# Chunked recurrence of a two-block transformer: the level products and their masked copies go over half of the columns

## The reference, cut to what matters

```python
def step(s, inp):
    qi, ki, vi, fi = inp
    a = jnp.cumsum(fi, axis=2)
    o_inter = jnp.einsum('bhtd,bhde->bhte', qi * jnp.exp(a), s)
    diff = a[:, :, :, None, :] - a[:, :, None, :, :]
    decay = jnp.exp(jnp.where(tri, diff, NEG_BIG))
    scores = jnp.einsum('bhtd,bhjd,bhtjd->bhtj', qi, ki, decay)
    o_intra = jnp.einsum('bhtj,bhje->bhte', scores, vi)
    ...
o_f, s_f = gla_chunk_scan(q, k_f, v, lf_f, s0_f)
o_b, s_b = gla_chunk_scan(rev(q), rev(k_b), rev(v), rev(lf_b), s0_b)
```

## Time and profile before

| | |
|---|---|
| median of 3 runs | 2542.26 us (2541.05 to 2546.97) |
| profiled execution: its own time | 2544.42 us |
| profiled execution: its span, first to last instruction | 2542.6 us |
| time around the span | 1.8 us |
| mean granted clock of TensorE | 0.990 |
| PE busy | 2449.7 us, 96% of the span |
| DVE busy | 1402.7 us, 55% |
| ACT busy | 1159.5 us, 46% |
| the recurrence, from first transposes to last `out` | about 1640 to 1964 us of the span |

### The profile page before, as it was taken

One profiled execution on the slowest core, in us unless ns is written; L12 is line 12 of the kernel. 1 busy time (PEld: TensorE's weight loads), 2 busy tenths in 40 slices (PEclk: granted clock), 3 DMA queues, 4 the chain that ended last, 5 costly groups with the idle time before them and its releaser, 6 DMA issues.

```text
span 2542.6 us, 30787 instructions
## 1 busy us (share of the span) xinstructions
PE 2449.7 (96%) x12116; PEld 1935.1 (76%) x12116; DVE 1402.7 (55%) x2264; ACT 1159.5 (46%) x1824; POOL 381.7 (15%) x307
## 2 busy tenths in 40 slices
PE   8999999999999999999999899999988998999998
PEld 6667678888877778888887677788777786788886
DVE  4787558758635456746765555354445433543443
ACT  4455654334445545434443766554555323442342
POOL 0001312112200002212212100011111211220221
PEclk9999999999999999999999999999999999899999
DMA  4122144434332224443522100110110332232331
GB/s 150 59 84 86 55 157 133 157 100 151 116 98 75 79 71 168 159 128 108 166 83 72 67 26 18 66 42 34 42 34 17 114 118 92 70 108 87 98 112 56
DMA packets 67439, 232.47 MB, mean 91 GB/s; under 512 B 7552, under 2 KB 7680, under 8 KB 66912
## 3 DMA queue, kind: packets, MB, share of 16 engines
q1 hardware_dynamic: 67296, 230.51, 28.3%
HBM read 226.21 MB, written 4.28 MB: 91 GB/s over the span
## 4 chain that ended last, share of the span: by engine, by line
PE 61%; ACT 6%; DVE 3%; issue 2%; POOL 0%; ACTq 0%; DVEq 0%
PE psum L424 17%; PE psum L426 16%; PE psum L425 16%; PE psum L2362 1%; PE psum L1004 1%; ACT SP L1052 1%; PE psum L977 1%; PE psum L1149 1%; ACT wH L409 1%; PE psum L1023 1%; PE psum L1160 1%; PE psum L1172 1%; PE psum L2329 1%; PE psum L2330 1%; DVE SP L1094 0%
## 5 line engine op out<-in xcount | busy, mean ns | idle before, releaser
L424 PE MATMUL psum<-hH,wH 128*128 128x512 f32 x1944 | 793.6, 408 | 32.8 <-DVE wL L414 10.7
L426 PE MATMUL psum<-hH,wL 128*128 128x512 f32 x1944 | 763.7, 393 | 0.0
L425 PE MATMUL psum<-hL,wH 128*128 128x512 f32 x1944 | 762.3, 392 | 0.0
L414 DVE TENSOR_TENSOR wL<-raw,wH 128x1024 fp32r<-128x1024 f32 (+2 forms) x358 | 454.2, 1269 | 456.7 <-ACT wH L409 455.9
L409 ACT ACTIVATE wH<-raw 128x1024 fp32r<-128x1024 f32 (+2 forms) x358 | 368.1, 1029 | 511.9 <-PE psum L426 510.8
L424 PEld LDWEIGHTS psum<-hH,wH 128*128 128x128 f32 x1944 | 366.7, 189 | 144.4 <-issue 41.1
L426 PEld LDWEIGHTS psum<-hH,wL 128*128 128x128 f32 x1944 | 366.8, 189 | 80.7
L425 PEld LDWEIGHTS psum<-hL,wH 128*128 128x128 f32 x1944 | 367.7, 189 | 67.7 <-issue 2.2
L424 PE MATMUL psum<-gH,wH 128*128 128x512 f32 x528 | 206.0, 390 | 0.0
L425 PE MATMUL psum<-gL,wH 128*128 128x512 f32 x528 | 205.4, 389 | 0.0
L426 PE MATMUL psum<-gH,wL 128*128 128x512 f32 x528 | 205.4, 389 | 0.0
(11 more groups left out here) (349 smaller groups left out, 3412.2 us busy)
## 6 DMA issues: line engine op xcount, KB each, us to landing
raw<-in_up SPq DMA_DIRECT2D x132, 512.0 KB, 3.4
raw<-in_dn SPq DMA_DIRECT2D x48, 704.0 KB, 4.1
raw<-in_win SPq DMA_DIRECT2D x56, 512.0 KB, 3.4
mbuf<-in_wmod SPq DMA_DIRECT2D x48, 512.0 KB, 3.5
raw<-in_we SPq DMA_DIRECT2D x33, 512.0 KB, 3.5
raw<-in_wq SPq DMA_DIRECT2D x24, 512.0 KB, 3.5
tm<-toep SPq DMA_DIRECT2D x32, 256.0 KB, 4.2
raw<-in_wo SPq DMA_DIRECT2D x32, 256.0 KB, 2.6
```

The lines of the kernel that those rows point to most:

```text
L414: ve.do.tensor_tensor(flat_of(wLb, n), flat_of(rawb, n), flat_of(wHb, n).bitcast(F), ALU.subtract).then_inc(*w_lo.up(n))
L424: pe.do.matmul(o, H[:, k, :], high(k), start=k == 0, stop=False)
L425: pe.do.matmul(o, H[:, k, :], low(k), start=False, stop=False)
L426: ins = pe.do.matmul(o, L[:, k, :], high(k), start=False, stop=k == kt - 1)
```

## The change: what it does

In `use` the moving operand is now only the query half of `Z` (`queries(...)`), 64 columns for each chunk in place of 128; the stationary operand is the whole chunk as before. The result goes densely into the first 256 columns of the bank (`half_scores(mat)`). The masked copy reads those 256 columns, and the query half of the mask, and writes into the query half of `scT`. On each of the five engines the same instructions stand in the same order, and no wait is added or removed; only these two change their shapes: PE's matmul from 128 to 64 moving columns, and DVE's masked copy from 128x512 to 128x256, in the views 4x64, 8x32, 16x16, 32x8, 64x4, 128x2 and 256 single elements. The copy of the diagonal (line 2510) stays at 128x512.

```diff
@@ pe_recurrence, "use"
                 for c in range(4):
-                    ins = pe.do.matmul(b128(pb, c), Z[z_][:, c, :], Z[z_][:, c, :], start=True, stop=True)
+
+                    ins = pe.do.matmul(half_scores(mat)[:, c, :, :], Z[z_][:, c, :], queries(Z[z_], mat, d)[:, c, :, :],
+                                       start=True, stop=True)
                 ins.then_inc(*g_pm.up((h, d, mat)))
@@ beside halves
     def halves(y, b_):
         return y.rearrange("p c (n u b) -> p c n u b", u=2, b=b_)
+
+    def queries(y, mat, d):
+
+        return halves(y, LEVELS[mat - 1])[:, :, :, (1, 0)[d], :]
+
+    def half_scores(mat):
+
+        return bank[2 + mat % 2][:, 0:256].rearrange("p (c n b) -> p c n b", c=4, b=LEVELS[mat - 1])
@@ ve_recurrence, "use"
-                ve.do.copy_predicated(scT, mask(2 * (mat - 1) + d), b3(bank[2 + mat % 2], 4)).then_inc(*g_cp.up(scored))
+                ve.do.copy_predicated(queries(scT, mat, d), queries(mask(2 * (mat - 1) + d), mat, d),
+                                      half_scores(mat)).then_inc(*g_cp.up(scored))
```

## The result

The changed kernel takes 2554.51 us (2545.73 to 2555.3, 11 runs) against 2542.6 us (2539.8 to 2546.97, 11 runs) of the kernel before, run beside it: ratio 1.0031, 95% interval 1.0018 to 1.0044, or 4.6 to 11.2 us more (the medians are 11.9 us apart, since that of the changed kernel lies in the upper of two groups). The forecast was 2540.1 us with a range of 2529 to 2548. Its times lie in two groups, 2545.7 to 2546.9 (5 runs) and 2554.5 to 2555.3 (6 runs); the profiled execution, 2554.51 us with a span of 2552.7 us, is of the upper one. The profile of before has a span of 2542.6 us, so the two traces are 10.1 us apart.

A forecast was written before the change was run, and what follows sets the result against it. PE, busy 96% of the span, was taken as the bound: its pace saves 0, eight shorter masked copies on its path save 2.2 us, so 2542.26 - 2.2 = 2540.1 us, range 2529 to 2548.

The forecast's parts named there:

- Rival C: Around PE's waits, half the columns make the granted clock fall more often, 1.7 us each, up to 2553.7 us; chance 0.09.
- 2.2 us for the copies: Path saving from 8 shorter masked copies: 1.6 us at ends of heads 0 to 2, 0.55 in head 3.
- PE's pace: In rows of eight, the weight load keeps each pair at about 0.111 us despite 64 columns; saving 0.
- Rival B: The matmul's columns set PE's pace in rows of eight: 2523.6 us, or 2530 to 2534 for paces between; chance 0.16.
- a record of about 220 ns: Sign for PE: one matmul's record some 50 ns shorter while starts stay 0.105 to 0.112 us apart.
- The masked copies: All 56 on DVE were to fall from 736 to 463 ns, alike in all seven views.
- the view of single elements: Sign against the copy estimate: masked copies in this view standing out above 600 ns.
- the whole 0.55 us goes through: At the ends of heads 0 to 2, two shorter copies ahead of `out` save 0.55 us a head.
- PE's wait ahead of `out`: Sign for the path: this wait at a head's end falls by some 0.3 us.
- the two waits with one copy of an earlier level in front: Head 3, first direction, waits at 1914.87 and 1920.62: one shorter copy each, 0.55 us saved together.
- DVE's busy time: Was to fall by about 15 us, 56 copies at 0.273 us, nearly all beside PE's projections.
- the wait of 0.74 us at 1707.03: PE's wait with one masked copy ahead of its `make`: 0.27 us shorter, giving nothing more in time.

The follow-up runs named there:

- e_prod_half: Kernel before with only the product halved to 64 moving columns, written into its places of the bank, under the whole copy: 2550.64 us, ratio 1.0034.
- e_full_dense: Changed kernel with the product over all 128 moving columns again, ordered by halves, the half copy kept: 2541.46 us, ratio 1.0001 to the kernel before.
- e_fill: Changed kernel plus ten unread matmuls of 512 columns in PE's wait at each head's start: 2543.07 us, ratio 1.0002 to the kernel before.
- e_thin_fills: Changed kernel plus unread matmuls in PE's waits, ten at each head's start and more in head 3: 2536.28 us, ratio 0.9976 to the kernel before.
- e_thin_starts: Changed kernel with 64 moving columns only in each head's first two rows, 128 by halves elsewhere: 2548.95 us, ratio 1.0022 to the kernel before.
- e_thin_end: Changed kernel with 64 moving columns only in the last four rows of head 3's second direction: 2546.84 us, ratio 1.0017 to the kernel before.
- e_stat64: Changed kernel with 64 stationary columns too, so half of the scores are not computed: one run, 2538.86 us.
- b_fill2: Kernel before plus ten unread matmuls of 512 columns ahead of each head's first product: 2539.25 us, ratio 0.9989 to the kernel before.
- e_target2: Changed kernel with 128 moving columns by halves and the copy's mask, source and target all dense, scores partly wrong: one run, 2539.63 us.
- e_copy_half: Kernel before with only the masked copy halved, the product over all 128 columns: 2543.09 us, ratio 1.0001 to the kernel before.
- e_mask_dense: Changed kernel with each mask stored by halves, so that the copy reads it densely: 2547.51 us, ratio 1.0027 to the kernel before.

## Why the prediction was wrong

**The step that failed** is the forecast's treatment of the clock. Rival C had the mechanism, the place ("with half the columns in each row of eight the array streams less just there") and the price ("each further fall costs 1.7 us", eight of them 2553.7 us); 11.9 us more loss are seven times that price, and the result is 2554.51. That its number came so near is in part luck: it counted eight new falls and took off 2.2 us for the copies, and the trace has one new fall (head 0's start), three falls of twice the length and one that is 10.2 us longer. Rival C got 0.09, by the argument "against it: the last rows of eight of a head, with short waits only, had 1.00 [...] and no wait becomes longer". Both halves of this are true and beside the point. The last rows of a head still have 1.00 (1700 to 1710 us above). No wait had to become longer: the waits of 2.5 us were there already, and three of four heads had a fall behind them. What changed is, for the most part, how long the fall lasts. The forecast asked only whether there would be more falls, priced at 1.7 us, and put the growth of those that were there at nothing; the runs show the falls of the starts of heads 1 to 3 costing 3.4 us each, and the one of head 3's end lasting from 1951 to 1969. That the product's columns cause it is shown (e_prod_half, e_full_dense), that it happens behind PE's waits too (e_fill, e_thin_fills), and that a few rows are enough (e_thin_starts, e_thin_end). How 64 columns in place of 128 keep the clock down is not shown.

**PE's pace** was right: 0.111 us a pair with 64 columns as with 128, and the load as its cause (e_stat64). Rival B is gone. The sign that was named for it, a record of about 220 ns, came only in part. One line's instructions, of the changed kernel's product (ns min/median/max):

```profile
L2363 PE MATMUL psum<-hf x256: 217/275/476, 1656.3 to 1964.0; 128*128 128x64 f32 x128
```

and of the kernel before:

```profile
L2362 PE MATMUL psum<-hf x256: 270/275/580, 1657.0 to 1957.6; 128*128 128x128 f32 x128
```

The shortest went from 270 to 217 ns, the 53 ns that the forecast gave to 64 columns; the median stays at 275: most records hold more than the time of their columns. The Trainium skill's figure of about 81 ns for a pair ("TensorE: Matmul & The Clock Gate", section "Back-to-back issue gap") was reached in no row of eight, with 128 moving columns or with 64; the trace doesn't agree.

**The masked copies** were right for levels 1 to 5 (0.44 us, forecast 0.463) and wrong for levels 6 and 7, which the forecast took to be alike since a pass of two operands over the same views takes 413 ns in the median. The prediction named the sign of it, "wrong if the view of single elements stands out above 600 ns". And just these two are on the path at each head's end. The chain of waits of the changed kernel there, which answers to the earlier trace rows:

```profile
1712.52 0.94 DVE f6r L2279
1713.46 0.66 DVE hf L2543
...
1714.21 0.74 DVE hf L2543
...
1714.99 0.49 PE psum L2371 x2
```

0.66 and 0.74 us, as they were. So "the whole 0.55 us goes through" became nothing: PE's wait ahead of `out` is 0.91 us, not 0.3 less. The periods say the same without the clock's noise: 81.97 and 82.01 in b_fill2 with whole copies and products, 82.04 in e_thin_fills with half ones. That the path was read rightly e_target2 shows. In head 3 the two waits with one copy of an earlier level in front did shorten, 1.78 and 0.66 us to 1.51 and 0.34:

```profile
1919.93 1.10 PE L2363 MATMUL psum<-ssum 128*128 128x64 f32 x8 [1.51 <-DVE ssum L2444]
...
1925.36 1.11 PE L2363 MATMUL psum<-hf 128*128 128x64 f32 x8 [0.34 <-DVE hf L2444]
```

Of the 2.2 us of the sum 0.6 were left.

**DVE's busy time** was to fall by about 15 us and fell by 5.1 (1402.7 to 1397.6). The copies gave 12.0 us (41.2 to 29.2), but the multiplications of `make` took 5.8 back. One of their two groups, of the kernel before and of the changed one:

```profile
L2434 DVE TENSOR_TENSOR ssum<-E,qt 128x256 f32<-128x256 f32 x24 | 10.5, 440 | 0.0
```

```profile
L2444 DVE TENSOR_TENSOR ssum<-E,qt 128x256 f32<-128x256 f32 x24 | 14.4, 601 | 0.0
```

The other group went from 417 to 475 ns. Behind a shorter copy DVE starts 19 of its 56 multiplications while POOL is still 0.43 to 0.56 us from the end of its own, and just these 19 take 0.71 to 0.85 us; the other 37 do not overlap POOL's and take about 0.42. Before, no overlap was over 0.26 us and none took over 0.53. The trace of e_copy_half shows the same 19. At one such place the shorter copy brings PE next to nothing: the wait of 0.74 us at 1707.03, which was to lose 0.27, became 0.68. The forecast put this lengthening at nothing. That POOL's work is the cause is read from this overlap; no run moved it.

**What stays open.** Why an execution has the long low stretch or not. The changed kernel's two groups are some 8.6 us apart, with mean clocks over the whole execution of 0.988 and 0.984; executions of before at 2546.8 to 2547.4 us were at 0.989. The heads' starts in the traces without filler and with 128 stationary columns say how far the columns settle it. With rows of 128 columns (before, e_copy_half, e_full_dense, e_thin_end, e_target2) 11 of 20 starts have a fall, ten of 3.4 us and one of 6.8. With rows of 64 (after, e_prod_half, e_thin_starts, e_mask_dense) 14 of 16 have one, nine of 6.8 us and five of 3.4; the fall at head 0's start is one of 3.4 us in all four. So thin rows make the long fall common and are neither enough for it nor needed. What decides within one kernel was not tried, nor were the thin rows behind waits of other lengths.

## What to carry to other kernels

Before taking columns out of matmuls that a weight load paces anyway, look at where those rows stand: behind a wait of PE, with a lower clock granted in the windows there, they make nothing quicker and can keep the clock down for longer. Price a fall of the clock by its length, and ask for each edit whether it makes an existing one longer, not only whether it adds one. A halved view buys its half only while its runs stay long: look at which of the views stands on the path, since it may be the one with runs of one element. And look at what the next pass then runs beside.

## What the runs showed of the hardware

- Behind PE's wait of 2.5 us at the starts of heads 1 and 2 (3.2 us at head 3) the clock, where it fell, was at 1.2 GHz for 3.4 us with rows of 128 columns in all cases but one (1.7 us lost) and, in three of the four profiles with 64 columns and no filler, for 6.8 us at all three starts. The Trainium skill tells of bursts between which PE is briefly idle, so that the loss is in falls and recoveries while a matmul at full clock keeps its duration ("TensorE: Matmul & The Clock Gate", section "A second HAM failure mode: psum-queue depth-cycling"); the trace agrees: at full clock the rows of both kernels are equally quick, and 11.9 us went to the clock.
- Filler in such waits pays by itself: ten matmuls of 512 columns, 2.44 us, four times, took 0.11% off the kernel before (95% interval 0.02 to 0.20%); with 20 more in head 3 the kernels with half copies came 0.23 to 0.24% below it.
- A masked copy of 256 elements took 0.44 us for runs of four elements and more in its target and 0.72 us for runs of two or one, as much as 512 elements in one dense pass; the stride of its byte mask cost nothing, and a two-operand pass over 256 elements with the same strides took 0.41 us in the median.
- A float32 pair of weight load and matmul took 0.111 us at full clock with 128 stationary columns, for 128 moving columns and for 64 alike, and 0.073 us with 64 of each.
- DVE's multiplication of 128x256 took 0.42 us by itself and 0.71 to 0.85 us where 0.43 us or more of it lay beside POOL's multiplication (after and e_copy_half, 19 of 56).
